# Latent attention's scores: rotary products over two heads at once from rounded high and low parts, and other tiles for the masks and maxima

## The chip, the cores and the metric

One core of a Trainium2 chip runs the whole program. The metric is the device time of one launch in microseconds (us); lower is better. A core has five engines that work side by side, each through its own list in order: PE (TensorE, matrix products; its weight loads are shown apart as PEld), DVE (VectorE), ACT (ScalarE), POOL (GpSimd) and SP (SyncE, which here starts transfers). They meet only by waiting on semaphores.

## The reference, cut to what matters

The kernel computes two layers of a decoder trunk over 256 positions (two blocks of 128). Each layer mixes four head groups, gates them, projects and normalises. The group that the change touches is latent attention with a rotary part:

```python
def _mla(c_q, c_kv, k_pe, ...):       # 4 heads
    q = (_rmsnorm(c_q, ...) @ w_uq)   # per head 128 plain + 64 rotary columns
    q = concat([q[..., :128], _rope(q[..., 128:], positions)])
    kv = (_rmsnorm(c_kv, ...) @ w_ukv)
    k_rot = _rope(k_pe, positions)    # one rotary key, shared by all heads
    k = concat([kv[..., :128], broadcast(k_rot)])
    return _causal_attention(q * (128 + 64) ** -0.5, k, v)   # mask, softmax, times v
```

So the scores of a head are a plain product over 128 features plus a rotary product over 64. All is float32, which PE takes in two ways: as float32, or from operands rounded to a format called fp32r. In the second way the kernel splits an operand into a rounded high part and the rest as a low part, and adds three products: high by high, low by high, high by low.

## The kernel before

**The stream.** Most of the work is a stream of weight tiles, 128 rows by 512 columns, numbered per layer by slot t. For each, SP loads two tiles at a time into `raw`; ACT writes the high part `hi` (L1073); DVE writes the low part `lo` = raw minus hi (L1414); PE multiplies: four 512-wide products with `hi` (L1327, L1328), then a wait for `lo`, then two with `lo` (L1331). `hi` and `lo` are rings of 5 places: a tile is split once PE has used the tile five slots before. A pair of raw tiles is loaded once `lo` of the pair four pairs earlier is written. Slots 144 to 159 are the chunk `rk`, 160 to 175 `rv`, 176 to 191 `z0`.

**The steps.** All else is hung between tiles by hand-written tables, `PE_AT`, `ACT_AT` and `DVE_AT`. A step at slot t runs on its engine right after that engine's own part of tile t, in the order in which the tables were filled. An engine that waits or works in a step keeps its next tile waiting. The steps that matter here, in the kernel before:

- PE, slot 156: `mla_scores` of heads 0 to 3. Per head four float32 products, for query block 0 (128 keys) and block 1 (256 keys) one plain (L1232) and one rotary (L1233). Each float32 product shows in the trace as two records.
- DVE, slots 161, 164, 173, 176: `mla_max` of a head: it adds the causal mask (L1807, 128x384), takes the two maxima (L1810, L1811) and scales them (L1812). Slots 165, 168, 177, 180: `mla_norm` (L1817, L1820). Slots 166, 169, 178, 181: `turn_head` (L1538), a transpose in 32x32 squares.
- ACT, slots 163, 166, 175, 178: `mla_exp` (L941) of a head, from DVE's maxima.
- DVE also has at 162 and 168 `cellT` (L1773, four 128-wide operations each), at 170 and 171 `rope_rk` of the two position blocks (L1783, L1784, L1800, 128x512 each), at 174 the transpose of `rk` (L1631).
- ACT, slots 150 and 151: `qrT` and `kpeT` copy the turned rotary queries and keys to `qrT` and `krT`, whose other halves hold zeros so that a pair of heads can share an operand.

**PE's order** is thus fixed by the program; nothing moves at run time but the moments.

Of the kernel before, what the change touches and what calls it, by code (L numbers as in the profile page):

```python
# [130 lines left out]
def _put(table, slot, *step):  # L131
    table.setdefault(slot, []).append(step)
# [30 lines left out]
for _h in range(HEADS):  # L163
    _put(ACT_AT, (78, 82, 88, 94)[_h], "mem_exp", _h)
    _put(ACT_AT, (102, 103, 110, 111)[_h], "mem_pT", _h)
    _put(ACT_AT, (163, 166, 175, 178)[_h], "mla_exp", _h)
for _s, *_step in [
# [29 lines left out]
for _h in range(HEADS):  # L197
    _put(DVE_AT, (76, 80, 86, 92)[_h], "mem_max", _h)
    _put(DVE_AT, (80, 84, 90, 96)[_h], "mem_norm", _h)
    _put(DVE_AT, (81, 85, 93, 97)[_h], "turn_head", "mem", _h)  # L200
    _put(DVE_AT, (103, 104, 111, 112)[_h], "lo", "mem_pT", _h)
    _put(DVE_AT, (161, 164, 173, 176)[_h], "mla_max", _h)
    _put(DVE_AT, (165, 168, 177, 180)[_h], "mla_norm", _h)
    _put(DVE_AT, (166, 169, 178, 181)[_h], "turn_head", "mla", _h)
for _s, *_step in [
        (20, "memv", 0), (22, "memv", 1),
        (36, "turn", "memk"), (211, "turn", "z3"), (228, "turn", "z2"), (45, "joined", "lx", 0), (53, "joined", "lx", 1),
        (61, "joined", "cq", 0), (69, "joined", "cq", 1),
        (237, "joined", "z1_", 0), (245, "joined", "z1_", 1),
        (110, "mem_out", 0), (118, "mem_out", 1),  # L210
        (123, "lo", "wukv", 0), (125, "lo", "wukv", 1), (128, "lo", "ckvT", 0),
        (54, "lo", "memk", 0), (56, "lo", "memk", 1), (63, "lo", "cq", 0), (71, "lo", "cq", 1),
        (86, "rms", 0), (88, "ckv", 0), (89, "kpe_rope", 0),
        (87, "gate_turn", 0), (95, "gates", 0), (99, "gate_scan", 0), (100, "gate_scan", 1), (101, "gate_scan", 2), (113, "ones", 0), (105, "gate_squares", 0),
        (102, "rms", 1), (107, "cqn", 0), (108, "cqn", 1), (109, "turn", "c"), (120, "cT", 0), (122, "cT", 1),
        (112, "ml_gap", 0), (113, "ml_gap", 1), (119, "ml_gap", 2), (120, "ml_gap", 3),
        (117, "ml_weigh", 0), (118, "ml_weigh", 1), (124, "ml_weigh", 2), (126, "ml_weigh", 3), (126, "skip", 0),
        (127, "ml_out", 0), (128, "ml_out", 1), (132, "ml_out", 2), (134, "ml_out", 3),
        (136, "cell_gate", 0), (137, "cell_gate", 1), (139, "cell_stats", 0), (140, "cell_stats", 1),
        (142, "cell_norm", 0), (144, "cell_norm", 1), (145, "turn", "cell"),  # L220
        (137, "q_rope", 0), (138, "q_rope", 1), (139, "turn_rotary", 0),
        (162, "cellT", 0), (168, "cellT", 1),
        (148, "rope_rq", 0), (150, "rope_rq", 1), (152, "turn", "rq"),
        (170, "rope_rk", 0), (171, "rope_rk", 1), (174, "turn", "rk"),
        (194, "mla_out", 0), (204, "mla_out", 1),
        (193, "ret_weigh", 0), (195, "ret_weigh", 1), (203, "ret_weigh", 2), (205, "ret_weigh", 3),
        (206, "ret_stats", 0), (208, "ret_norm", 0), (212, "ret_stats", 1), (214, "ret_norm", 1), (215, "ret_gate", 0), (216, "turn", "ret"),
        (229, "gate", 3, 0), (230, "gate", 3, 1), (242, "gate", 2, 0), (243, "gate", 2, 1),
        (244, "gate", 1, 0), (248, "gate", 1, 1),
        (232, "y_lo", 0), (233, "y_lo", 1), (235, "y_lo", 2), (237, "y_lo", 3),  # L230
        (246, "y_lo", 4), (247, "y_lo", 5), (252, "y_lo", 6), (253, "y_lo", 7)]:
    _put(DVE_AT, _s, *_step)
# [82 lines left out]
def build_trunk(nc, a, out):  # L315
    ctx = ExitStack()
    with ctx:
        def sb(name, shape, dt=F32):
            return ctx.enter_context(nc.sbuf_tensor(name, shape, dt))

        def signal(name, per_layer, before=0, step=1):
            return Signal(ctx.enter_context(nc.semaphore(name)), per_layer, before, step)
# [32 lines left out]
        gcol, freq = sb("gcol", [P, 4, HEADS]), sb("freq", [P, FR + FM])  # L355
        B, Br = zip(*(row_of[i] for i in range(10)))
        qr = sb("qr", [P, NT, HEADS * ROT])
        qrT = sb("qrT", [P, 2, SEQ])
        krr = sb("krr", [P, NT, P])
        krT = sb("krT", [P, 2, SEQ])  # L360
        prob = sb("prob", [P, 2, 512])
        pTl = sb("pTl", [P, 2, 512], F32R)
        with nc.sbuf_tensor("pTh", [P, 2, 512], F32R) as pTh:
# [137 lines left out]
        normed = signal("normed", 0)  # L501
        x_hi, x_lo = signal("x_hi", 8), signal("x_lo", 8)
        y_hi, y_lo = signal("y_hi", 8), signal("y_lo", 8)
        kv_split, uq_split = signal("kv_split", 3), signal("uq_split", 4)
        hi_part = signal("hi_part", len(HI_STEPS))
        conv_done, xc_done = signal("conv_done", 1), signal("xc_done", 2)
        lx_pad = signal("lx_pad", 1)
# [315 lines left out]
        def _(act):  # L823
# [20 lines left out]
            for l in range(DEPTH):  # L844
# [172 lines left out]
                def kpeT(_):  # L1017
                    wait_turned(act, l, "rot")
                    for r in range(2):
                        half_ = slice(r * ROT, (r + 1) * ROT)  # L1020
                        m = act.activation(krT[half_, r, :].rearrange("p (i a r) -> p i a r", i=NT, a=4),
                                           rot_blocks[half_, 4:6], ACT.Copy)
                    m.then_inc(rotary_turned.sem, 1)

# [69 lines left out]
        def _(pe):  # L1094
# [5 lines left out]
            for l in range(DEPTH):  # L1100
# [122 lines left out]
                def mla_scores(h):
                    if h == 0:
                        wait_read(pe, l, ("mla_kn", 0), ("mla_kn", 1), ("mla_qn", 0), ("mla_qn", 1))
                        pe.wait_ge(rotary_turned.sem, rotary_turned.at(l, 1))
                        pe.wait_ge(ready.sem, 3)
                        stand_alone(pe)
                    o = take("mla_scores", h)
                    for i, (c0, c1) in enumerate(((0, P), (P, TRI))):  # L1230
                        q = slice(i * P, (i + 1) * P)
                        pe.matmul(o[:, c0:c1], qnT[:, h, q], knT[:, h, 0:c1 - c0], start=True, stop=False)  # L1232
                        m = pe.matmul(o[:, c0:c1], qrT[:, h // 2, q], krT[:, h % 2, 0:c1 - c0], start=False, stop=True)  # L1233
# [154 lines left out]
        def _(dve):  # L1388
            dve.memset(tmp[:, 0:P], 1.0).then_inc(ready.sem, 1)
            dve.memset(half[:, :], -0.5).then_inc(ready.sem, 1)  # L1390
            dve.memset(krT[ROT:P, 0, :], 0.0)
            dve.memset(krT[0:ROT, 1, :], 0.0).then_inc(ready.sem, 1)
            for p in range(2):
                dve.sem_inc(acc_read[p].sem, 2)
            for b in range(NBANK):
# [40 lines left out]
            for l in range(DEPTH):  # L1436
# [88 lines left out]
                def turn_head(name, h):  # L1525

                    dve.wait_ge(prob_done.sem, prob_done.at(l, h + (HEADS if name == "mla" else 0)))
                    if (name, h) == ("mem", 0):
                        wait_job(dve, l, ("ml_fold", 0))
                    group = f"{name}{h // 2}"  # L1530
# [273 lines left out]
                def mla_max(h):

                    wait_job(dve, l, ("mla_scores", h))
                    dve.tensor_tensor(prob[:, h % 2, 0:TRI], bank(l, ("mla_scores", h))[:, 0:TRI], tri, ALU.add)\  # L1807
                       .then_inc(free_bank(l, "mla_scores", h), 1)
                    wait_read(dve, l, ("mla_scores", h))
                    dve.tensor_reduce(nmax[:, h % 2, 0:1], prob[:, h % 2, 0:P], AX.X, ALU.max, negate=True)  # L1810
                    link(dve.tensor_reduce(nmax[:, h % 2, 1:2], prob[:, h % 2, P:TRI], AX.X, ALU.max, negate=True))  # L1811
                    dve.tensor_scalar(nmax[:, h % 2, :], nmax[:, h % 2, :], MLA_SCALE, None, ALU.mult)\  # L1812
                       .then_inc(max_done.sem, 1)
# [64 lines left out]
                def residual(c, *only):  # L1878
# [8 lines left out]
                    for i in only or range(NT):  # L1887
# [166 lines left out]
```

## Time and profile before

| | us |
|---|---|
| median of 3 runs | 891.05 (890.68 to 891.11) |
| the profiled execution | 892.54 |
| its span, first to last instruction | 890.7 |
| PE busy (TensorE, 4532 instructions) | 883.3, 99% |
| DVE busy | 661.7, 74% |
| ACT busy | 487.7, 55% |
| granted TensorE clock, mean | 1.000 (2.4 GHz) |

A product on PE is pipelined: its row in the timeline lasts longer than the distance to the next start, so the work is read from starts, not from durations. Short operations on DVE and ACT overlap a little in the same way. A number in square brackets at the end of a timeline row is the idle time before it, with what ended it.

### The profile page before, as it was taken

How to read it: one execution, taken by the hardware profiler on the slowest of the kernel's cores; microseconds unless marked ns; L12 is line 12 of the kernel's file. 1: busy time of each engine (PE TensorE's matmuls, PEld its weight loads, DVE VectorE, ACT ScalarE, POOL GpSimd, SP SyncE). 2: the span in 40 equal slices, each digit the busy share in tenths (PEclk: the TensorE clock that was granted, in tenths of full speed). 3: DMA queues.
4: the chain of work that ended last, by engine and by line, in shares of the span. 5: the costliest groups of instructions: out<-in, count | busy, mean ns of one | idle time of the engine just before them, and what ended most of it. 6: DMA issues, size and time to landing. Idle time of an engine off the chain costs nothing.

```text
span 890.7 us, 13196 instructions
## 1 busy us (share of the span) xinstructions
PE 883.3 (99%) x4532; PEld 758.4 (85%) x4532; DVE 661.7 (74%) x1322; ACT 487.7 (55%) x914; POOL 18.0 (2%) x18
## 2 busy tenths in 40 slices
PE   9999999999999999999999999999999999999997
PEld 7888998788888888888888889888888888888896
DVE  6869697777595667766668887878777978777765
ACT  6656776445455346544476557746354553565541
POOL 0000000000000000000000000000000001000001
PEclk9999999999999999999999999999999999999999
DMA  9796587547669688666665965885485874978832
GB/s 358 283 326 210 137 264 247 185 143 216 217 212 319 213 243 271 192 198 196 193 192 173 312 243 155 280 267 157 145 267 154 272 236 153 289 209 265 322 95 95
DMA packets 70962, 198.23 MB, mean 223 GB/s; under 512 B 9448, under 2 KB 23024, under 8 KB 70256
## 3 DMA queue, kind: packets, MB, share of 16 engines
q1 hardware_dynamic: 70320, 196.34, 68.6%
q10 hardware_dynamic: 576, 1.05, 0.4%
q8 instruction: 36, 0.59, 0.3%
q14 instruction: 30, 0.25, 0.1%
HBM read 182.38 MB, written 14.95 MB: 222 GB/s over the span
## 4 chain that ended last, share of the span: by engine, by line
PE 92%; DMA 3%; issue 1%; DVE 1%; SPq 1%; ACT 1%; POOL 0%; POOLq 0%; ACTq 0%; DVEq 0%
PE acc L1327 23%; PE acc L1328 23%; PE acc L1331 23%; PE acc L1342 10%; PE acc L1348 5%; DMA B<-turn 1%; PE work L1116 1%; PE work L1115 1%; PE work L1114 1%; DMA raw<-in_w 1%; DMA turn<-B 1%; DMA B<-in_mem_t 1%; PE work L1233 1%; PE work L1232 1%; SPq L761 1%
## 5 line engine op out<-in xcount | busy, mean ns | idle before, releaser
L1414 DVE TENSOR_TENSOR lo<-raw,hi 128x512 fp32r<-128x512 f32 (+2 forms) x607 | 387.8, 656 | 185.5 <-ACT hi L1073 177.0
L1073 ACT ACTIVATE hi<-raw 128x512 fp32r<-128x512 f32 (+2 forms) x607 | 355.7, 603 | 295.3 <-PE acc L1331 229.5
L1327 PE MATMUL acc<-hi,xx 128*128 128x512 f32 (+2 forms) x768 | 285.6, 375 | 1.0 <-ACT hi L1073 1.0
L1328 PE MATMUL acc<-hi,xx 128*128 128x512 f32 (+2 forms) x768 | 283.6, 372 | 0.0
L1331 PE MATMUL acc<-lo,xx 128*128 128x512 f32 (+2 forms) x768 | 223.0, 372 | 0.0
L1327 PEld LDWEIGHTS acc<-hi,xx 128*128 128x128 f32 x768 | 144.6, 188 | 25.0 <-ACT hi L1073 1.4
L1328 PEld LDWEIGHTS acc<-hi,xx 128*128 128x128 f32 x768 | 144.6, 188 | 23.6
L1331 PEld LDWEIGHTS acc<-lo,xx 128*128 128x128 f32 x768 | 140.4, 188 | 24.6
L1342 PE MATMUL acc<-xx,hi 128*128 128x512 f32 x384 | 96.1, 392 | 0.0
L1342 PEld LDWEIGHTS acc<-xx,hi 128*128 128x128 f32 x384 | 69.3, 189 | 12.6
L1348 PEld LDWEIGHTS acc<-xx,lo 128*128 128x128 f32 x384 | 52.4, 190 | 3.7
L1348 PE MATMUL acc<-xx,lo 128*128 128x256 f32 x384 | 53.5, 282 | 0.0
L1327 PE MATMUL acc<-hi,mm 128*128 128x512 f32 x126 | 49.5, 393 | 0.6 <-DVE mm L1420 0.6
L1328 PE MATMUL acc<-hi,mm 128*128 128x512 f32 x126 | 49.1, 389 | 0.0
L1331 PE MATMUL acc<-lo,mm 128*128 128x512 f32 x126 | 38.8, 389 | 0.0
L1327 PEld LDWEIGHTS acc<-hi,mm 128*128 128x128 f32 x126 | 23.7, 188 | 5.7 <-DVE mm L1420 1.0
L1331 PEld LDWEIGHTS acc<-lo,mm 128*128 128x128 f32 x126 | 23.7, 188 | 5.0
L1328 PEld LDWEIGHTS acc<-hi,mm 128*128 128x128 f32 x126 | 23.7, 188 | 4.7
L799 POOL TENSOR_TENSOR rstd<-stats,half 128x4 f32<-128x4 f32 (+1 forms) x6 | 9.6, 1593 | 351.0 <-DVE stats L1842 221.6
L976 ACT ACTIVATE B<-work 128x512 f32<-128x512 f32 x12 | 7.2, 596 | 14.7 <-PE work L1116 14.7
L941 ACT ACTIVATE prob<-prob,nmax 128x128 f32<-128x128 f32 (+1 forms) x16 | 7.2, 448 | 10.3 <-DVE nmax L1812 10.3
L1580 DVE SCALAR_TENSOR_TENSOR B<-B,cols 128x256 f32<-128x256 f32 x24 | 11.6, 483 | 0.6
(345 smaller groups left out, 967.5 us busy)
## 6 DMA issues: line engine op xcount, KB each, us to landing
raw<-in_w SPq DMA_DIRECT2D x263, 512.0 KB, 4.4
B<-turn SPq DMA_DIRECT2D x80, 128.0 KB, 4.4
raw<-in_w SPq DMA_DIRECT2D x26, 256.0 KB, 2.7
turn<-B SPq DMA_DIRECT2D x12, 512.0 KB, 6.0
raw<-in_w SPq DMA_DIRECT2D x16, 328.0 KB, 3.3
turn<-Y SPq DMA_DIRECT2D x8, 512.0 KB, 5.4
Y<-in_wuq SPq DMA_DIRECT2D x2, 1152.0 KB, 8.7
Y<-in_x_t SPq DMA_DIRECT2D x4, 512.0 KB, 8.3
```

The source lines that it names most:

```text
L761: sp.dma_start(turn_to[name][b * 32:(b + 1) * 32, :].rearrange("c (a n) -> c a n", a=4), a["turn"][TURNS.index(name), :, b * n:(b + 1) * n ...
L799: return pool.tensor_tensor(dst, src, half[:, 0:n], ALU.pow)
L1073: act.activation(place(l, t, hi), raw[:, s, (t % 2) * w:(t % 2 + 1) * w], ACT.Copy)\
L1114: pe.matmul(o, ah, bh, start=start, stop=False)
L1115: pe.matmul(o, al, bh, start=False, stop=False)
L1327: pe.matmul(o, ah[:, q], hi[:, s, 0:w], start=k == 0, stop=False, skip_group_check=name == "memv")
L1328: pe.matmul(o, al[:, q], hi[:, s, 0:w], start=False, stop=False, skip_group_check=name == "memv")
L1331: m = pe.matmul(acc[:, p, i, 0:w], ah[:, i * P:(i + 1) * P], lo[:, s, 0:w], start=False, stop=k == KT - 1, skip_group_check=name == "memv")
L1342: pe.matmul(acc[:, p, j, :], hi[:, (l * SLOTS + t + u) % RING, q], x, start=k + u == 0 and kk == 0, stop=False, skip_group_check=True)
L1348: m = pe.matmul(acc[:, p, j, 0:SEQ], lo[:, s, q], both_parts[:, 2 * k + kk, 0, :], start=False, stop=2 * k + kk == KT - 1, skip_group_chec ...
L1414: dve.tensor_tensor(place(l, t, lo), raw[:, s, (t % 2) * w:(t % 2 + 1) * w], place(l, t, hi).bitcast(F32), ALU.subtract).then_inc(lo_done. ...
L1580: m = dve.scalar_tensor_tensor(xcT[:, j, :], LX[:, j, tap:tap + SEQ], wcol, xcT[:, j, :], ALU.mult, ALU.add)
```

## The change

Five things, each in both layers:

- The rotary operands become fp32r pairs: ACT's copies write `qrh` (in the buffer `pTh`) and `krh`, and a new DVE step `rot_lo` at slot 153 writes the low parts `qrl` (in `pTl`) and `krl`.
- PE's rotary products take two heads at once. A bank of PSUM now holds two heads of one query block instead of one head of two blocks: per bank three fp32r products, 256 wide for block 0 and 512 wide for block 1. Then the plain products follow, float32 as before.
- `mla_max` works on a bank, so on two heads of one block: mask and maxima, and after the second block the scaling of both heads.
- The tables move: `mla_max` from 161, 164, 173, 176 to 161, 162, 170, 171; `mla_exp` from 163, 166, 175, 178 to 164, 166, 172, 174; `mla_norm` from 165, 168, 177, 180 to 166, 168, 174, 177; the transposes to 167, 169, 175, 178.
- Two more memsets at the start, and three waits: `qrT` for an old job, `turn_head` of head 2 for the transpose of `rk`, `mla_max` 2 for the transposes of heads 0 and 1.

```diff
-    _put(ACT_AT, (163, 166, 175, 178)[_h], "mla_exp", _h)
+    _put(ACT_AT, (164, 166, 172, 174)[_h], "mla_exp", _h)
-    _put(DVE_AT, (161, 164, 173, 176)[_h], "mla_max", _h)
+    _put(DVE_AT, (161, 162, 170, 171)[_h], "mla_max", _h)
...
+(153, "rot_lo", 0),
...
+                        pe.wait_ge(kv_split.sem, kv_split.at(l, 3))
...
+                        for b in range(HEADS):
+                            (q, i), o = divmod(b, 2), take("mla_scores", b)
+                            w = (i + 1) * P
+                            o = o[:, 0:2 * w].rearrange("p (h k) -> p h k", h=2)
+                            (ah, al), (bh, bl) = (... qrh, qrl), (... krh, krl)
+                            pe.matmul(o, ah, bh, start=True, stop=False, skip_group_check=True)
+                            pe.matmul(o, al, bh, start=False, stop=False, skip_group_check=True)
+                            pe.matmul(o, ah, bl, start=False, stop=False, skip_group_check=True)
...
+                    for h in (2 * q, 2 * q + 1):
+                        m = pe.matmul(o[:, h % 2 * w:(h % 2 + 1) * w], qnT[:, h, i * P:(i + 1) * P], knT[:, h, 0:w],
+                                      start=False, stop=True, skip_group_check=True)
...
+                def rot_lo(_):
+                    dve.wait_ge(rotary_turned.sem, rotary_turned.at(l, 1))
+                    wait_job(dve, l, ("mla_v", 1))
+                    dve.tensor_tensor(at(qrl), rot_blocks[:, 0:4], at(qrh).bitcast(F32), ALU.subtract)
+                    for r in range(2):
+                        m = dve.tensor_tensor(at(krl), rot_blocks[half_, 4:6], at(krh).bitcast(F32), ALU.subtract)
+                    m.then_inc(kv_split.sem, 1)
...
+                def mla_max(n):
+                    i, c0, c1 = n % 2, n % 2 * P, P + n % 2 * 2 * P
+                    wait_job(dve, l, ("mla_scores", n))
+                    dve.tensor_tensor(prob[:, :, c0:c1], o, tri[:, c0:c1]..., ALU.add)
+                    link(dve.tensor_reduce(nmax[:, :, i], prob[:, :, c0:c1], AX.X, ALU.max, negate=True))
+                    if i:
+                        for h in range(2):
+                            dve.tensor_scalar(nmax[:, h, :], nmax[:, h, :], MLA_SCALE, None, ALU.mult)
```

On PE, at the end of slot 156, stood before (the first two heads of four; `B` are the plain operands, `acc` rows are the stream):

```order
L1232 MATMUL work<-B 128x128
L1233 MATMUL work<-krT,qrT 128x128
L1232 MATMUL work<-B 128x256
L1233 MATMUL work<-krT,qrT 128x256
L1232 MATMUL work<-B 128x128
L1233 MATMUL work<-krT,qrT 128x128
L1232 MATMUL work<-B 128x256
L1233 MATMUL work<-krT,qrT 128x256
```

and stands now (the first two banks' rotary products, which come twice, then all the plain ones):

```order
L1235 MATMUL work<-krh,pTh 128x256
L1236 MATMUL work<-krh,pTl 128x256
L1237 MATMUL work<-krl,pTh 128x256
L1235 MATMUL work<-krh,pTh 128x512
L1236 MATMUL work<-krh,pTl 128x512
L1237 MATMUL work<-krl,pTh 128x512
...
L1242 MATMUL work<-B 128x128 x2
L1242 MATMUL work<-B 128x256 x2
```

Eight float32 rotary products became twelve fp32r ones; the plain ones only moved behind them.

On DVE, from tile 170 on, stood before (`lo` is the low part of a tile, `Y` and `tmp` with `cos` and `sin` the steps `rope_rk`, `prob` and `nmax` the step `mla_max`):

```order
L1414 TENSOR_TENSOR lo<-raw,hi 128x512
L1783 TENSOR_TENSOR Y<-acc,cos 128x512
L1784 TENSOR_TENSOR tmp<-acc,sin 128x512
L1800 TENSOR_TENSOR Y<-Y,tmp 128x512
L1414 TENSOR_TENSOR lo<-raw,hi 128x512
L1783 TENSOR_TENSOR Y<-acc,cos 128x512
L1784 TENSOR_TENSOR tmp<-acc,sin 128x512
L1800 TENSOR_TENSOR Y<-Y,tmp 128x512
L1414 TENSOR_TENSOR lo<-raw,hi 128x512 x2
L1807 TENSOR_TENSOR prob<-work,const 128x384
```

and stands now:

```order
L1426 TENSOR_TENSOR lo<-raw,hi 128x512
L1837 TENSOR_TENSOR prob<-work,const 128x2x128
L1840 TENSOR_REDUCE nmax<-prob 128x2
L1797 TENSOR_TENSOR Y<-acc,cos 128x512
...
L1426 TENSOR_TENSOR lo<-raw,hi 128x512
L1837 TENSOR_TENSOR prob<-work,const 128x2x256
L1840 TENSOR_REDUCE nmax<-prob 128x2
L1843 TENSOR_SCALAR nmax<-nmax 128x2 x2
L1797 TENSOR_TENSOR Y<-acc,cos 128x512
...
L1426 TENSOR_TENSOR lo<-raw,hi 128x512 x3
```

The masks and maxima of heads 2 and 3 moved ahead of the two `rope_rk` steps, so they now stand between the low parts of tiles 170 and 172.

On ACT, around the exponentials of latent attention, stood before (`hi` is the high part of a tile, `prob,rsum` the step `mla_exp`):

```order
L1073 ACTIVATE hi<-raw 128x512 x12
L941 ACT_TABLE_LOAD
L941 ACTIVATE prob,rsum<-prob,nmax 128x128
L941 ACTIVATE prob,rsum<-prob,nmax 128x256
L1073 ACTIVATE hi<-raw 128x512 x3
L941 ACTIVATE prob,rsum<-prob,nmax 128x128
L941 ACTIVATE prob,rsum<-prob,nmax 128x256
L1073 ACTIVATE hi<-raw 128x512 x9
```

and stands now:

```order
L1075 ACTIVATE hi<-raw 128x512 x13
L942 ACT_TABLE_LOAD
L942 ACTIVATE prob,rsum<-prob,nmax 128x128
L942 ACTIVATE prob,rsum<-prob,nmax 128x256
L1075 ACTIVATE hi<-raw 128x512 x2
L942 ACTIVATE prob,rsum<-prob,nmax 128x128
L942 ACTIVATE prob,rsum<-prob,nmax 128x256
L1075 ACTIVATE hi<-raw 128x512 x6
```

The first exponential moved one tile later, behind `hi` of tile 164; the third came from behind tile 175 to behind tile 172.

## Rows read from the trace of the kernel before

**Rows 1.** PE's waits over the span: who for whom, us, times, longest.
```profile
PE acc L1327 <- ACT hi L1073: 1.0, 1, 1.0
```

**Rows 2.** PE's timeline, slots 156 and 157, then 172: start us, us, work.
```profile
227.74 0.62 PE L1331 MATMUL acc<-lo,xx 128*128 128x512 f32 x2
228.19 0.38 PE L1232 MATMUL work<-B 128*128 128x128 f32 x2
...
228.63 0.60 PE L1232 MATMUL work<-B 128*128 128x256 f32 x2
229.07 0.59 PE L1233 MATMUL work<-krT,qrT 128*128 128x256 f32 x2
229.50 0.38 PE L1232 MATMUL work<-B 128*128 128x128 f32 x2
...
234.35 0.62 PE L1331 MATMUL acc<-lo,xx 128*128 128x512 f32 x2
...
254.75 0.62 PE L1331 MATMUL acc<-lo,xx 128*128 128x512 f32 x2
```

**Rows 3.** PE's timeline, 18 fp32r products 256 wide, and the next.
```profile
186.21 0.28 PE L1114 MATMUL work<-Xr 128*128 128x256 f32 x1
...
188.36 0.40 PE L1327 MATMUL acc<-hi,xx 128*128 128x512 f32 x1
```

**Rows 4.** DVE's timeline, slots 153 to 172 of layer 1.
```profile
220.30 1.86 DVE L1414 TENSOR_TENSOR lo<-raw,hi 128x512 fp32r<-128x512 f32 x3
...
235.73 0.69 DVE L1414 TENSOR_TENSOR lo<-raw,hi 128x512 fp32r<-128x512 f32 x1 [4.62 <-ACT hi L1073]
...
240.46 0.55 DVE L1807 TENSOR_TENSOR prob<-work,const 128x384 f32<-128x384 f32 x1
...
241.25 0.41 DVE L1811 TENSOR_REDUCE nmax<-prob 128x1 f32<-128x256 f32 x1
241.69 0.17 DVE L1812 TENSOR_SCALAR nmax<-nmax 128x2 f32<-128x2 f32 x1
...
244.13 1.25 DVE L1414 TENSOR_TENSOR lo<-raw,hi 128x512 fp32r<-128x512 f32 x2
...
247.61 0.57 DVE L1538 STREAM_TRANSPOSE Y<-prob 128x384 f32<-128x384 f32 x1
248.10 0.66 DVE L1414 TENSOR_TENSOR lo<-raw,hi 128x512 fp32r<-128x512 f32 x1
248.68 0.69 DVE L1783 TENSOR_TENSOR Y<-acc,cos 128x512 f32<-128x512 f32 x1
...
250.72 0.69 DVE L1414 TENSOR_TENSOR lo<-raw,hi 128x512 fp32r<-128x512 f32 x1
...
253.37 1.29 DVE L1414 TENSOR_TENSOR lo<-raw,hi 128x512 fp32r<-128x512 f32 x2
```

**Rows 5.** ACT's timeline, slots 162 to 166.
```profile
235.06 0.63 ACT L1073 ACTIVATE hi<-raw 128x512 fp32r<-128x512 f32 x1 [6.04 <-PE acc L1331]
...
237.01 1.28 ACT L941 ACT_TABLE_LOAD   x1
...
239.20 1.14 ACT L1073 ACTIVATE hi<-raw 128x512 fp32r<-128x512 f32 x2
240.50 0.63 ACT L1073 ACTIVATE hi<-raw 128x512 fp32r<-128x512 f32 x1 [0.16 <-PE acc L1331]
```

**Rows 6.** The tile `nmax`: durations in ns, min, median, max.
```profile
L1544 DVE TENSOR_REDUCE nmax<-work x8: 680/682/685, 101.6 to 559.0; 128x2 f32<-128x512 f32 x8
```

**Rows 7.** ACT's and PE's timelines where PE waits for a high part.
```profile
165.04 1.13 ACT L1073 ACTIVATE hi<-raw 128x512 fp32r<-128x512 f32 x2
...
165.71 0.50 PE L1327 MATMUL acc<-hi,xx 128*128 128x512 f32 x1 [1.02 <-ACT hi L1073]
166.05 0.40 PE L1328 MATMUL acc<-hi,xx 128*128 128x512 f32 x1
```

**Rows 8.** DVE's timeline, slot 172 of layer 2.
```profile
691.04 1.29 DVE L1414 TENSOR_TENSOR lo<-raw,hi 128x512 fp32r<-128x512 f32 x2
```

More of the change, by code:

```diff
@@ L201 @@
     _put(DVE_AT, (103, 104, 111, 112)[_h], "lo", "mem_pT", _h)
-    _put(DVE_AT, (161, 164, 173, 176)[_h], "mla_max", _h)
-    _put(DVE_AT, (165, 168, 177, 180)[_h], "mla_norm", _h)
-    _put(DVE_AT, (166, 169, 178, 181)[_h], "turn_head", "mla", _h)
+    _put(DVE_AT, (161, 162, 170, 171)[_h], "mla_max", _h)
+    _put(DVE_AT, (166, 168, 174, 177)[_h], "mla_norm", _h)
+    _put(DVE_AT, (167, 169, 175, 178)[_h], "turn_head", "mla", _h)
 for _s, *_step in [
@@ L222 @@
         (162, "cellT", 0), (168, "cellT", 1),
-        (148, "rope_rq", 0), (150, "rope_rq", 1), (152, "turn", "rq"),
+        (148, "rope_rq", 0), (150, "rope_rq", 1), (152, "turn", "rq"), (153, "rot_lo", 0),
         (170, "rope_rk", 0), (171, "rope_rk", 1), (174, "turn", "rk"),
@@ L357, in build_trunk @@
         qr = sb("qr", [P, NT, HEADS * ROT])
-        qrT = sb("qrT", [P, 2, SEQ])
+        krl = sb("krl", [P, 2, SEQ], F32R)
         krr = sb("krr", [P, NT, P])
-        krT = sb("krT", [P, 2, SEQ])
+        krh = sb("krh", [P, 2, SEQ], F32R)
         prob = sb("prob", [P, 2, 512])
@@ L409, in build_trunk @@
         ckvp = pTl[:, 0, 0:SEQ], pTl[:, 0, SEQ:2 * SEQ]
+        qrh, qrl = (x[:, 0, :] for x in (pTh, pTl))
         gap = Y[:, 4096 - 2 * TRI:4096].rearrange("p (b c) -> p b c", b=2)
@@ L503, in build_trunk @@
         y_hi, y_lo = signal("y_hi", 8), signal("y_lo", 8)
-        kv_split, uq_split = signal("kv_split", 3), signal("uq_split", 4)
+        kv_split, uq_split = signal("kv_split", 4), signal("uq_split", 4)
         hi_part = signal("hi_part", len(HI_STEPS))
@@ L1020, in kpeT @@
                         half_ = slice(r * ROT, (r + 1) * ROT)
-                        m = act.activation(krT[half_, r, :].rearrange("p (i a r) -> p i a r", i=NT, a=4),
+                        m = act.activation(krh[half_, r, :].rearrange("p (i a r) -> p i a r", i=NT, a=4),
                                            rot_blocks[half_, 4:6], ACT.Copy)
@@ L1030, in qrT_ @@
                     wait_turned(act, l, "rot")
-                    act.activation(qrT[:, :, :].rearrange("p j (i a r) -> p (j i) a r", i=NT, a=4), rot_blocks[:, 0:4], ACT.Copy)\
+                    wait_job(act, l, ("ml_out", HEADS - 1))
+                    act.activation(qrh.rearrange("p (n a r) -> p n a r", n=4, a=4), rot_blocks[:, 0:4], ACT.Copy)\
                        .then_inc(rotary_turned.sem, 1)
@@ L1221, in mla_v, with mla_scores @@
                             both(wukvp, lambda x: x[:, :, 1, :])).then_inc(job_done.sem, 1)
[L1223 to L1226, printed above, removed]
+                def mla_scores(n):
+                    if n == 0:
+                        pe.wait_ge(kv_split.sem, kv_split.at(l, 3))
                         pe.wait_ge(ready.sem, 3)
                         stand_alone(pe)
[L1229 to L1233, printed above, removed]
+                        for b in range(HEADS):
+                            (q, i), o = divmod(b, 2), take("mla_scores", b)
+                            w = (i + 1) * P
+                            o = o[:, 0:2 * w].rearrange("p (h k) -> p h k", h=2)
+                            (ah, al), (bh, bl) = (x[:, q * SEQ + i * P:q * SEQ + (i + 1) * P] for x in (qrh, qrl)),                                                  (x[:, :, 0:w] for x in (krh, krl))
+                            pe.matmul(o, ah, bh, start=True, stop=False, skip_group_check=True)
+                            pe.matmul(o, al, bh, start=False, stop=False, skip_group_check=True)
+                            pe.matmul(o, ah, bl, start=False, stop=False, skip_group_check=True)
+                        wait_read(pe, l, ("mla_kn", 0), ("mla_kn", 1), ("mla_qn", 0), ("mla_qn", 1))
+                    (q, i), o = divmod(n, 2), bank(l, ("mla_scores", n))
+                    w = (i + 1) * P
+                    for h in (2 * q, 2 * q + 1):
+                        m = pe.matmul(o[:, h % 2 * w:(h % 2 + 1) * w], qnT[:, h, i * P:(i + 1) * P], knT[:, h, 0:w],
+                                      start=False, stop=True, skip_group_check=True)
                     m.then_inc(job_done.sem, 1)
@@ L1390, in _ @@
             dve.memset(half[:, :], -0.5).then_inc(ready.sem, 1)
-            dve.memset(krT[ROT:P, 0, :], 0.0)
-            dve.memset(krT[0:ROT, 1, :], 0.0).then_inc(ready.sem, 1)
+            for part in (krl, krh):
+                dve.memset(part[ROT:P, 0, :].bitcast(F32), 0.0)
+                m = dve.memset(part[0:ROT, 1, :].bitcast(F32), 0.0)
+            m.then_inc(ready.sem, 1)
             for p in range(2):
@@ L1527, in turn_head @@
                     dve.wait_ge(prob_done.sem, prob_done.at(l, h + (HEADS if name == "mla" else 0)))
+                    if (name, h) == ("mla", 2):
+                        dve.wait_ge(squared["rk"].sem, squared["rk"].at(l, 0))
                     if (name, h) == ("mem", 0):
@@ L1802, in rope_ret @@
                     return go
[L1804 to L1813, printed above, removed]
+                def rot_lo(_):
+                    dve.wait_ge(rotary_turned.sem, rotary_turned.at(l, 1))
+                    wait_job(dve, l, ("mla_v", 1))
+                    at = lambda x: x.rearrange("p (n a r) -> p n a r", n=4, a=4)
+                    dve.tensor_tensor(at(qrl), rot_blocks[:, 0:4], at(qrh).bitcast(F32), ALU.subtract)
+                    for r in range(2):
+                        half_ = slice(r * ROT, (r + 1) * ROT)
+                        at = lambda x: x[half_, r, :].rearrange("p (i a r) -> p i a r", i=NT, a=4)
+                        m = dve.tensor_tensor(at(krl), rot_blocks[half_, 4:6], at(krh).bitcast(F32), ALU.subtract)
+                    m.then_inc(kv_split.sem, 1)
@@ new lines, in mla_max @@
+                def mla_max(n):
+                    i, c0, c1 = n % 2, n % 2 * P, P + n % 2 * 2 * P
+                    wait_job(dve, l, ("mla_scores", n))
+                    if n == 2:
+                        dve.wait_ge(squared["mla0"].sem, squared["mla0"].at(l, 1))
+                    o = bank(l, ("mla_scores", n))[:, 0:2 * (c1 - c0)].rearrange("p (h k) -> p h k", h=2)
+                    dve.tensor_tensor(prob[:, :, c0:c1], o, tri[:, c0:c1].unsqueeze(1).to_broadcast([P, 2, c1 - c0]), ALU.add)\
+                       .then_inc(free_bank(l, "mla_scores", n), 1)
+                    wait_read(dve, l, ("mla_scores", n))
+                    link(dve.tensor_reduce(nmax[:, :, i], prob[:, :, c0:c1], AX.X, ALU.max, negate=True))
+                    if i:
+                        for h in range(2):
+                            dve.tensor_scalar(nmax[:, h, :], nmax[:, h, :], MLA_SCALE, None, ALU.mult)\
+                               .then_inc(max_done.sem, 1)
@@ L1897, in _ @@
                          "q_rope": q_rope, "rope_rq": rope_ret("rq", rqt, 0), "rope_rk": rope_ret("rk", rkt, 2),
-                         "mla_max": mla_max, "mla_norm": mla_norm, "mla_out": out_pair("mla_out", mlao),
+                         "rot_lo": rot_lo, "mla_max": mla_max, "mla_norm": mla_norm, "mla_out": out_pair("mla_out", mlao),
                          "ret_weigh": ret_weigh, "ret_stats": ret_stats, "ret_norm": ret_norm,
```

## The prediction

> **What bounds the kernel now.** First the list of waits: PE is busy 99% of the span, and it waits for another engine inside the layers once, 1.0 us [rows 1]. So every microsecond of PE's own list is a microsecond of the kernel, and work on DVE and ACT costs nothing until it makes PE wait. Then PE's timeline: a tile of the stream has six 512-wide products and starts every 1.36 us (tile 157's low products start at 234.35, tile 172's, 15 tiles on, at 254.75: 20.40 / 15) [rows 2]. Then the same tiles on DVE: the low part of tile 172 starts at 253.37 and lasts 0.69, so it is written at 254.06 against a need at 254.75 [rows 2, 4]. Here DVE is 0.69 us ahead of PE, no more; from 244.13 to 253.37 it runs one operation behind another. In layer 2 the same row stands 437.67 us later [rows 8], so one walk serves for both layers.
>
> **What PE saves.** The block at slot 156 takes 234.35 - 227.74 - 1.36 = 5.25 us [rows 2]. A 128-wide float32 product takes half of 228.63 - 228.19, so 0.22, and a 256-wide one 0.44 (228.63 to 229.07 the plain one, to 229.50 the rotary one) [rows 2]. The rotary half, four of each, is 4 x 0.655 = 2.62 us, and goes. In come six fp32r products 256 wide and six 512 wide. The first kind takes (188.36 - 186.21) / 18 = 0.119 us [rows 3], the second 1.36 / 6 = 0.227. That is 0.72 + 1.36 = 2.08. Saved per layer: 0.54 us, for both 1.08. The block becomes 4.71 us. The plain products keep their number, shape and kind, so I cost their move at nothing; changes between the two kinds of product cost nothing to be seen before, since 4 x 1.31 already fills the block.
>
> On the 256-wide product the row shows 0.119 us. The Trainium skill ("TensorE: Matmul & The Clock Gate", section on the back-to-back issue gap) gives width / 2.4 + 2.5 ns, 109 ns for this width, where only the products count; the trace does not agree by 10 ns. By that rule the estimate would be a saving 0.06 us larger per layer.
>
> **What is added and hidden.** `rot_lo` after tile 153's low part: three subtractions, at most 0.69 for the 512-wide one and 0.42 for each of the others, 1.5 us. Tile 153's low part starts at 220.30 [rows 4], so the step ends by 222.5, and tile 154's low part by 223.2. PE needs that at 227.74 - 2 x 1.36 = 225.02 and the new operands at 228.19. Both are covered by about 2 us or more; without that cover it would cost up to 1.5 us a layer. The two memsets stand in DVE's first microseconds, while it waits for the first tiles. ACT's copies keep their shapes. SP's list is the same.
>
> **The schedule after slot 156.** PE's times are now 0.54 earlier: low products of tile 157 at 233.81, of tile 172 at 254.21. DVE must be followed up to there.
>
> ACT sets where it starts. Before, `hi` of tile 162 runs at 235.06 and of tile 166 at 240.50, each as PE frees a place of the ring, 1.36 a tile [rows 5]. So `hi` of 164 would run at 235.06 + 2 x 1.36 = 237.78 before, 237.24 now. Behind it now come the table load and the first exponential: 2.19 from 237.01 to 239.20 [rows 5], less the load's 1.28 gives 0.91 for an exponential alone. So: `hi` 164 at 237.24, table load at 237.89 (0.65 later, as before), `hi` 165 at 240.08, 166 and the second exponential about 0.53 apart, and 0.91 later `hi` 167 at 242.04. Its low part follows 0.67 later, as 235.73 follows 235.06 [rows 4, 5]: tile 167 on DVE at 242.71. DVE's own list alone would bring it there at 242.6, so the start is held from two sides.
>
> From there DVE does not rest. Before, 244.13 to 248.10 is tile 167, tile 168, norm, `cellT`, tile 169, transpose: 3.97 [rows 4]. The same six follow now, with one more transpose in between (247.61 to 248.10, 0.49), then tile 170's low part (0.58): 242.71 + 3.97 + 0.49 + 0.58 = 247.75. Before, that point was 248.68 [rows 4], which is 248.14 on PE's new clock. So DVE is 0.39 better off here, because one `mla_max` has moved into the idle time ahead of tile 163.
>
> Now the moved steps. `mla_max` 2: a mask of 256 elements and a reduce of 256. The mask of 384 takes 0.55, the 512-wide operation from PSUM 0.69, so 256 takes 0.42, plus 0.03 to the dependent one; the reduce of 256 takes 0.44 start to start [rows 4]. Sum 0.89: 248.64. `rope_rk` 0 takes 250.72 - 248.68 = 2.04 [rows 4]: 250.68. Tile 171: 0.61, 251.29. `mla_max` 3: mask of 512, 0.69 + 0.03; reduce of 512; two scalings, 0.17 each, overlapping by 0.1 as neighbours do here, 0.16 or more. The trace has no reduce of 512 from SBUF. From below the 256-wide row, 0.41; from above 0.90, twice 0.44 [rows 4]; I take the 512-wide reduce from PSUM, 0.68 [rows 6], plus 0.02. Sum 1.58: 252.87. `rope_rk` 1: 254.91. Tile 172's low part lasts 0.69: written at 255.60.
>
> PE needs it at 254.21. When PE really waits, it loses a little more: the high part at 165.04 takes 0.62 and ends at 165.66, yet the product behind the waiting one starts at 166.05, so the waiting one ran from 165.82, 0.16 after the operand [rows 7]. So tile 172's low products run at 255.76: **a wait of 1.55 us in each layer.**
>
> Behind it nothing else is late. Tiles 173 and 174 follow at 0.6, written by 256.8; norm 0.65, transpose of `rk` 1.17 (1.24 long), and tile 175 is written near 259.3, with PE's need at 255.76 + 3 x 1.36 = 259.84. ACT waits for the maxima until 252.9, runs the third exponential, and has `hi` of 173 at 254.4; PE needs it at 256.2. The wait is behind `hi` 173 and 174 only.
>
> On the reduce the row shows 0.68 from PSUM, and the subtraction from SBUF takes 0.69, the operation from PSUM at 248.68 the same 0.69 [rows 4]. The Trainium skill ("VectorE: DVE Perf Modes", section on the errata) gives 58 cycles plus the width for a source in SBUF and 120 for one in PSUM, at 0.96 GHz: 0.59 us for the new reduce. The trace does not agree with that difference. By the rule the estimate of the wait would be about 0.1 us shorter in each layer, the sign of the result the same.
>
> **The sum.** Per layer -0.54 + 1.55 = +1.01; both layers +2.0. The profiled execution has 892.54 us around a span of 890.7; its changed counterpart comes to 892.7 in span and 894.6 in all. The median of the runs is 1.49 below the profiled execution; on it, 891.05 + 2.0 = **893.1 us**. The reduce alone moves this by -0.6 to +0.4 (its bounds, twice), and the point where DVE starts its dense stretch by 0.2 either way per layer.
>
> A change of 0.2%, 1.8 us, is what a measurement can tell; the edges are 889.3 and 892.8.
>
> **Rivals.**
>
> *Only the saving shows.* DVE's low part of tile 172 comes in time, and the kernel takes 891.05 - 1.08 = 890.0. For it: PE's block is sure to shrink, and the new form does less mask work over a layer (2.5 for two heads against 2 x 1.31). Against it: DVE had 0.69 us before tile 172 and now has about 2.5 us of masks and maxima before it that stood after it, less the 0.39 + 0.54 gained. And even if tile 172 were in time, tile 175 comes with norm and transpose behind it at 259.3 against 258.29, so about 1 us of wait would come there. Chance 8%, and within 0.2%. Faster by more than 0.2% needs another 0.7 us saved by PE; 4%.
>
> *The wait is there but smaller,* by DVE operations that overlap more than their rows before (0.1 us each at ten joints). Then the wait is 0.9 to 1.4 us, and the time 891.8 to 892.8, within 0.2%. Chance 22%.
>
> *A second wait.* ACT stands still for the maxima up to tile 172's exponential, so `hi` of tiles 173 and 174 and behind them the reloads of `raw` come late. That decides from the point where DVE's scaling ends after 254.7 (then `hi` 173 is written after 256.2). Then every further 0.1 on DVE costs PE 0.1, and with the reload's transfer late too it would be about 1 us a layer more: 895. By the walk there is 1.8 us of room. Chance 5%.
>
> *The change does not do what it says:* the rotary products at fp32r cost more than read, for instance 256-wide at the 512-wide price, 6 x 0.11 = 0.65 a layer. Then nothing is saved and the time is 894.4. Against it stand 18 such products in a row at 0.119 [rows 3]. Chance 4%.
>
> The forecast itself, 892.8 to 893.7, has the rest, 57%. Faster 0.04; same 0.08 + 0.22 = 0.30; slower 0.66. Range 891.7 to 894.1: it leaves out the first rival and the dearest ones.
>
> **What would show it.** In the changed profile: the time from the last low product of tile 156 to tile 157's low products shrinks by 0.54; twelve rows of `krh`/`krl` at 0.12 and 0.23. A new wait of PE at a low product (L1341) for DVE, once in each layer, about 1.4 to 1.6 us, some 27.5 us after the block begins. DVE without idle time for the 13 us before it. ACT idle about 3.5 us for `nmax` before the third exponential. Wrong would be: no wait at tile 172, the wait at another tile, or one for ACT or a transfer.

## The result, and the profile after

| | before | changed |
|---|---|---|
| median | 890.91 us (890.53 to 891.88, 12 runs) | 892.76 us (892.58 to 894.01, 12 runs) |
| profiled execution, its span | 892.54, 890.7 | 892.74, 890.9 |

The ratio is 1.0023, with a 95% interval of 1.0015 to 1.0030: the change made the kernel slower by 1.85 us (1.3 to 2.7). The forecast was 893.1 in a range of 891.7 to 894.1, with 0.66 on slower by more than 0.2%. The ratio measured lies just past that edge of 1.002, and its interval reaches below it: that the kernel became slower is clear, that it became slower by more than 0.2% is not.

**The new wait.** The list of PE's waits in the changed kernel (who for whom: us in total, times, longest) answers to [rows 1]:

```profile
PE acc L1341 <- DVE lo L1426: 2.5, 2, 1.3
PE work L1100 <- DVE half L1400: 1.1, 1, 1.1
PE acc L1313 <- ACT hi L1067: 0.5, 1, 0.5
PE acc L1393 <- ACT tmp L1087: 0.3, 1, 0.3
```

The first row is new: twice, once in each layer, PE stands at low products until DVE has written the low part of a tile. All others are at the program's start and end. The row's 1.3 us is less than what PE loses, since a product's row reaches on into the wait. The starts tell it better. PE's timeline around the block and at tile 172 answers to [rows 2]:

```profile
225.84 0.61 PE L1341 MATMUL acc<-lo,xx 128*128 128x512 f32 x2
226.30 0.28 PE L1235 MATMUL work<-krh,pTh 128*128 128x256 f32 x1
226.41 0.28 PE L1236 MATMUL work<-krh,pTl 128*128 128x256 f32 x1
226.53 0.28 PE L1237 MATMUL work<-krl,pTh 128*128 128x256 f32 x1
226.65 0.40 PE L1235 MATMUL work<-krh,pTh 128*128 128x512 f32 x1
226.88 0.40 PE L1236 MATMUL work<-krh,pTl 128*128 128x512 f32 x1
...
228.40 2.78 PE L1242 MATMUL work<-B 128*128 128x128 f32 x16
...
231.94 0.62 PE L1341 MATMUL acc<-lo,xx 128*128 128x512 f32 x2
...
252.11 0.39 PE L1338 MATMUL acc<-hi,xx 128*128 128x512 f32 x1
253.77 0.73 PE L1341 MATMUL acc<-lo,xx 128*128 128x512 f32 x2 [1.27 <-DVE lo L1426]
254.34 0.40 PE L1337 MATMUL acc<-hi,xx 128*128 128x512 f32 x1
```

The block: 231.94 - 225.84 - 1.36 = 4.74 us, against 5.25 before, so 0.51 saved. Rotary products start every 0.12 us (256 wide) and 0.23 us (512 wide). The wait: tile 172 is the fifteenth after tile 157, and its low products were due at 231.94 + 15 x 1.36 = 252.34. They started at 253.77, and since the next product comes 0.57 later where two take 0.455, they ran from 253.88: 1.54 us lost. In layer 2 the same pair of starts, 690.85 and 692.50, gives 1.53.

DVE's timeline before that wait answers to [rows 4] (`x3` in a row are three tiles' operations put together):

```profile
240.78 0.69 DVE L1426 TENSOR_TENSOR lo<-raw,hi 128x512 fp32r<-128x512 f32 x1
...
245.26 0.65 DVE L1426 TENSOR_TENSOR lo<-raw,hi 128x512 fp32r<-128x512 f32 x1
245.83 0.41 DVE L1837 TENSOR_TENSOR prob<-work,const 128x256 f32<-128x256 f32 x1
246.28 0.42 DVE L1840 TENSOR_REDUCE nmax<-prob 128x2 f32<-128x256 f32 x1
246.73 0.69 DVE L1797 TENSOR_TENSOR Y<-acc,cos 128x512 f32<-128x512 f32 x1
...
248.78 0.69 DVE L1426 TENSOR_TENSOR lo<-raw,hi 128x512 fp32r<-128x512 f32 x1
249.39 0.68 DVE L1837 TENSOR_TENSOR prob<-work,const 128x512 f32<-128x512 f32 x1
250.11 0.69 DVE L1840 TENSOR_REDUCE nmax<-prob 128x2 f32<-128x512 f32 x1
250.83 0.24 DVE L1843 TENSOR_SCALAR nmax<-nmax 128x2 f32<-128x2 f32 x2
250.98 0.68 DVE L1797 TENSOR_TENSOR Y<-acc,cos 128x512 f32<-128x512 f32 x1
...
253.02 1.90 DVE L1426 TENSOR_TENSOR lo<-raw,hi 128x512 fp32r<-128x512 f32 x3
```

No row from 240.78 to 253.02 carries idle time. Tile 172's low part starts at 253.02 and is written at 253.71; PE's weight load for the waiting product starts at 253.77.

**Why the two spans differ by 0.2 only.** The profiled execution of the kernel before had a wait that this one has not: PE for a high part at 165.71 [rows 1, 7]. By its starts that cost 1.29 us; the program's start took the rest. So PE stood 1.89 us earlier here (226.30 against 228.19) before anything of the change had run. The source of that wait is a transfer (into the buffer `B`) that a step on DVE waited for:

```profile
163.23 0.69 DVE L1687 TENSOR_TENSOR B<-B,cols 128x512 f32<-128x512 f32 x1 [2.77 <-DMA B<-turn]
```

ACT then waited for DVE's result before it could write the next high part. This wait comes and goes. In the profiles where DVE waited for that transfer 2.8, 2.8, 2.5, 2.4 and 2.0 us in one layer, PE lost 1.29, 1.34, 1.06, 0.88 and 0.54 us by its starts; where it waited 1.5 us or less, PE lost nothing there. The profiles of the kernel before and of its variant below have it, and three of the seven profiles of the changed kernel and its variants. The execution profiled before was 1.6 us above its median, this one is at its median. So the medians carry the result, and the profiles the mechanism: 2 x (1.54 - 0.51) = 2.1 us, against 1.85 between the medians. The 0.2 us between the two are not explained; the interval of 1.3 to 2.7 us holds both.

### The profile page after: what moved, and what is told of

Same layout as the page of the kernel before. It is cut to its first block, busy times and chain, and to the rows that moved or that the text cites. A ratio compares the mean times of both kernels' runs of the same rounds, so it can differ in the third digit from the quotient of the medians.

```text
span 890.9 us, 13190 instructions
## 1 busy us (share of the span) xinstructions
PE 882.2 (99%) x4524; PEld 756.8 (85%) x4524; DVE 665.0 (75%) x1322; ACT 488.4 (55%) x914; POOL 18.0 (2%) x18
## 4 chain that ended last, share of the span: by engine, by line
PE 94%; DVE 3%; issue 1%; ACT 1%; DMA 0%; POOL 0%; POOLq 0%; ACTq 0%; DVEq 0%
PE acc L1341 23%; PE acc L1337 23%; PE acc L1338 23%; PE acc L1352 10%; PE acc L1358 5%; PE work L1118 1%; PE work L1117 1%; PE work L1116 1%; DVE lo L1426 1%; PE work L1242 1%; DMA B<-in_mem_t 0%; PE work L1111 0%; PE work L1265 0%; PE work L1254 0%; PE work L1174 0%
## 5 line engine op out<-in xcount | busy, mean ns | idle before, releaser
L1338 PE MATMUL acc<-hi,B1r 128*128 128x512 f32 (+1 forms) x32 | 12.0, 377 | 0.0
```

What stands on the lines that cost most here:

```text
L1338: pe.matmul(o, al[:, q], hi[:, s, 0:w], start=False, stop=False, skip_group_check=name == "memv")
```

## The experiments

All were timed against the kernel before on the same chip, whose median was 890.72 us for the first four and 890.94 for the other three.

**Masks and maxima of heads 2 and 3 late.** Only the tables differ from the changed kernel:

```diff
-    _put(ACT_AT, (164, 166, 172, 174)[_h], "mla_exp", _h)
+    _put(ACT_AT, (164, 166, 177, 178)[_h], "mla_exp", _h)
-    _put(DVE_AT, (161, 162, 170, 171)[_h], "mla_max", _h)
-    _put(DVE_AT, (166, 168, 174, 177)[_h], "mla_norm", _h)
-    _put(DVE_AT, (167, 169, 175, 178)[_h], "turn_head", "mla", _h)
+    _put(DVE_AT, (161, 162, 173, 175)[_h], "mla_max", _h)
+    _put(DVE_AT, (166, 168, 178, 180)[_h], "mla_norm", _h)
+    _put(DVE_AT, (167, 169, 179, 181)[_h], "turn_head", "mla", _h)
```

> The changed kernel with heads 2 and 3 late: mla_max at 173 and 175 instead of 170 and 171, mla_exp at 177 and 178, mla_norm at 178 and 180, the transposes at 179 and 181. Theory (the whole loss is PE's wait for the low part of tile 172, behind the moved masks and maxima): that wait is gone. By the walk on DVE, with PE's clock as in the prediction, the low part of tile 172 is written at 253.1 against a need at 254.05, tile 175 at 257.0 against 258.1, tile 176 at 259.15 against 259.5. What is left is PE's shorter block, 0.51 us a layer: 1.0 us under the kernel before, about 889.9, ratio 0.9989. Rival (the loss lies in the new products or in the subtractions of rot_lo, and the tables do nothing): as the changed kernel, 892.8.

Measured: 889.65 us (889.46 to 890.35, 11 runs), ratio 0.9987 (0.9978 to 0.9996). PE's waits in its profile are those at the start and the end alone:

```profile
PE work L1100 <- DVE half L1400: 1.1, 1, 1.1
PE acc L1393 <- ACT tmp L1087: 0.3, 1, 0.3
PE acc L1313 <- ACT hi L1067: 0.3, 1, 0.3
```

What is left is PE's saving, 1.07 us. With the time of `rot_lo` twice below this is the lowest, ahead of both kernels; the rival that laid the loss on the new products falls.

**The tables alone.** The kernel before, its own products and its `mla_max` by head, with heads 2 and 3 at the change's slots, and two waits to keep shared buffers in order:

```diff
-    _put(ACT_AT, (163, 166, 175, 178)[_h], "mla_exp", _h)
-    _put(DVE_AT, (161, 164, 173, 176)[_h], "mla_max", _h)
-    _put(DVE_AT, (165, 168, 177, 180)[_h], "mla_norm", _h)
-    _put(DVE_AT, (166, 169, 178, 181)[_h], "turn_head", "mla", _h)
+    _put(ACT_AT, (163, 166, 172, 174)[_h], "mla_exp", _h)
+    _put(DVE_AT, (161, 164, 170, 171)[_h], "mla_max", _h)
+    _put(DVE_AT, (165, 168, 174, 177)[_h], "mla_norm", _h)
+    _put(DVE_AT, (166, 169, 175, 178)[_h], "turn_head", "mla", _h)
```

> The kernel before with its own products, masks and maxima by head, but with heads 2 and 3 at the slots of the changed kernel: mla_max 170 and 171, mla_exp 172 and 174, mla_norm 174 and 177, the transposes 175 and 178. Theory: DVE reaches tile 170 as before; two mla_max of 1.32 us now stand ahead of tile 172. Low part written at 248.68 + 2 x (1.32 + 2.04) + 0.61 + 0.69 = 256.7, plus 0.16 to the product, against 254.75: a wait of 2.1 us in each layer, 4.2 us over the kernel before, about 895.1, ratio 1.0047. Rival (tables do nothing): 890.9.

Measured: 896.72 us (896.63 to 897.17, 5 runs), ratio 1.0065 (1.0053 to 1.0078), 6.0 us over the kernel before. The direction and the place were right, the size was 1.8 us short. PE's timeline in layer 1:

```profile
253.26 0.39 PE L1328 MATMUL acc<-hi,xx 128*128 128x512 f32 x1
255.48 1.04 PE L1331 MATMUL acc<-lo,xx 128*128 128x512 f32 x2 [1.82 <-DVE lo L1414]
256.31 0.63 PE L1327 MATMUL acc<-hi,xx 128*128 128x512 f32 x1
256.74 0.63 PE L1328 MATMUL acc<-hi,xx 128*128 128x512 f32 x1
257.17 0.63 PE L1327 MATMUL acc<-hi,xx 128*128 128x512 f32 x1
257.59 0.63 PE L1328 MATMUL acc<-hi,xx 128*128 128x512 f32 x1
258.02 1.05 PE L1331 MATMUL acc<-lo,xx 128*128 128x512 f32 x2
258.87 0.51 PE L1327 MATMUL acc<-hi,xx 128*128 128x512 f32 x1
259.23 0.40 PE L1328 MATMUL acc<-hi,xx 128*128 128x512 f32 x1
```

The wait is 255.59 - (253.26 + 0.23) = 2.1 us, as expected. But behind it eight products take 3.39 us, 0.42 each instead of 0.227, and the ninth 0.36. That stretch by engine (us, PE busy (x), granted clock, DMA share, GB/s):

```profile
255.48:258.87 3.39, 3.39 (x8) 0.53 0.58 195
```

The granted clock fell to half, the level of 1.2 GHz. Summed over the stretch this costs 1.6 us. In layer 2 of the same execution the wait was as long, and the clock stayed. So 2 x 2.1 + 1.6 = 5.8 of the 6.0 us. All five executions had a mean clock of 0.997 or 0.998, where those of the kernel before had 0.999 or 1.000, so the fall came in each of them.

**The last reduce twice.** In `mla_max`, for the last bank only:

```diff
                     link(dve.tensor_reduce(nmax[:, :, i], prob[:, :, c0:c1], AX.X, ALU.max, negate=True))
+                    if n == 3:
+                        link(dve.tensor_reduce(nmax[:, :, i], prob[:, :, c0:c1], AX.X, ALU.max, negate=True))
```

> The changed kernel with the last reduce of mla_max (heads 2 and 3, second block, 512 elements) run twice, once per layer more. Theory: the second one, 0.72 us from start to start, goes whole into PE's wait at tile 172, which grows from 1.55 to 2.27 us: 1.4 us over the changed kernel, about 894.2, ratio to the kernel before 1.0038. Rival (DVE is not what PE waits for at that place, or has room): as the changed kernel, 892.8.

Measured: 895.78 us, but spread from 894.31 to 897.67 over 5 runs, ratio 1.0056 (1.0043 to 1.0070). The wait behaved as said: in layer 2 the products before it and after it are

```profile
694.10 0.39 PE L1338 MATMUL acc<-hi,xx 128*128 128x512 f32 x1
696.46 0.74 PE L1341 MATMUL acc<-lo,xx 128*128 128x512 f32 x2 [1.98 <-DVE lo L1426]
```

so 696.57 - 694.33 = 2.24 us, 0.7 more than in the changed kernel. In layer 1 the half clock came again (granted clock 0.52 from 254.39 to 257.88) and took 1.6 us:

```profile
254.39 1.22 PE L1341 MATMUL acc<-lo,xx 128*128 128x512 f32 x2 [1.98 <-DVE lo L1426]
255.41 0.63 PE L1337 MATMUL acc<-hi,xx 128*128 128x512 f32 x1
```

The lowest run, 894.31, is what DVE's time alone gives (894.2); the others lie 1.4 to 3.4 above it. The mean clock of each execution goes with this: 0.999 in the lowest, 0.997 in the three at 895.67 to 896.73, and 0.995 in the one at 897.67, which is what a fall in both layers would give; that execution has no timeline.

**The last masks and maxima one slot later.**

```diff
-    _put(ACT_AT, (164, 166, 172, 174)[_h], "mla_exp", _h)
-    _put(DVE_AT, (161, 162, 170, 171)[_h], "mla_max", _h)
+    _put(ACT_AT, (164, 166, 173, 174)[_h], "mla_exp", _h)
+    _put(DVE_AT, (161, 162, 170, 172)[_h], "mla_max", _h)
```

> The changed kernel with only its last mla_max and the third exponential one slot later (172 and 173). Theory, by the walk: tile 172's low part is written at 254.0, just in time (need 254.05), but the masks and maxima now hold tile 173: written at 256.2, plus 0.16, against 255.57, a wait of 0.8 us; behind it norm and transpose of rk hold tile 175: 259.4 against 259.1, 0.3 us more. Sum 1.1 us a layer instead of 1.55: 2 x (1.1 - 0.51) = 1.2 us over the kernel before, about 892.1, ratio 1.0013. A reading in which the place alone decides (behind tile 172 is free): 889.9. Rival (tables do nothing): 892.8.

Measured: 893.92 us (893.73 to 894.82, 6 runs), ratio 1.0033 (1.0020 to 1.0045): slower than the changed kernel, where I expected it faster. PE's timeline:

```profile
253.42 0.62 PE L1341 MATMUL acc<-lo,xx 128*128 128x512 f32 x2
...
254.57 0.40 PE L1338 MATMUL acc<-hi,xx 128*128 128x512 f32 x1
255.43 0.73 PE L1341 MATMUL acc<-lo,xx 128*128 128x512 f32 x2 [0.47 <-DVE lo L1426]
256.31 0.50 PE L1337 MATMUL acc<-hi,xx 128*128 128x512 f32 x1
...
258.51 0.40 PE L1338 MATMUL acc<-hi,xx 128*128 128x512 f32 x1
259.42 0.73 PE L1341 MATMUL acc<-lo,xx 128*128 128x512 f32 x2 [0.52 <-DVE lo L1426]
```

Tile 172 (253.42) is in time and tile 173 late by 0.76, both as the walk had it. Then comes what it missed: tile 174's first product (256.31) runs 0.43 late, waiting for its high part, and the list of PE's waits does not show it. ACT stood at the third exponential, and wrote it late:

```profile
254.75 0.40 ACT L942 ACTIVATE prob<-prob,nmax 128x128 f32<-128x128 f32 x1 [5.49 <-DVE nmax L1843]
...
255.64 0.61 ACT L1075 ACTIVATE hi<-raw 128x512 fp32r<-128x512 f32 x1
```

DVE in turn waited 0.91 us for that high part, and tile 175 came 0.79 late where I had 0.3. The sum is 0.76 + 0.43 + 0.79 = 1.98 us a layer, and 2 x (1.98 - 0.51) = 2.9 of the measured 3.2.

**`rot_lo` twice,** on top of the late masks: its three subtractions in a loop of two, with a wait between.

```diff
+                    for again in range(2):
                         dve.tensor_tensor(at(qrl), rot_blocks[:, 0:4], at(qrh).bitcast(F32), ALU.subtract)
...
+                        if again == 0:
+                            link(m)
```

> The kernel of the run before with the late masks, with the subtractions of rot_lo run twice, one after the other: about 1.5 us more of DVE work at slot 153 in each layer. Theory (rot_lo is wholly hidden, with about 2 us of room before tile 154's low part and 5 before the products that use it): no wait of PE there, the time of late_masks, 889.7. Rival (rot_lo is on the path, or near it): up to 3 us more, 892.7.

Measured: 889.66 us (889.40 to 889.82, 11 runs), the time of the late masks to 0.01. Once, the step takes 1.48 us on DVE in the changed kernel (218.98 to 220.46), and even twice it is hidden: PE has no wait in the layers of that profile.

**Exponentials late, masks where the change put them.**

```diff
-    _put(ACT_AT, (164, 166, 172, 174)[_h], "mla_exp", _h)
-    _put(DVE_AT, (166, 168, 174, 177)[_h], "mla_norm", _h)
-    _put(DVE_AT, (167, 169, 175, 178)[_h], "turn_head", "mla", _h)
+    _put(ACT_AT, (164, 166, 177, 178)[_h], "mla_exp", _h)
+    _put(DVE_AT, (166, 168, 178, 180)[_h], "mla_norm", _h)
+    _put(DVE_AT, (167, 169, 179, 181)[_h], "turn_head", "mla", _h)
```

> The changed kernel with its masks and maxima where the change put them (170, 171), but exponentials, norms and transposes of heads 2 and 3 late (ACT 177, 178; DVE 178, 180 and 179, 181). Theory (PE waits for DVE's low part of tile 172 alone, and ACT's standing still for the maxima is covered): the same wait of 1.55 us in each layer at tile 172, 892.6, ratio 1.0021. Rival (ACT's stop at tile 172 has a share in it): less than that, down to 889.7 if it is all.

Measured: 892.74 us (892.64 to 894.88, 11 runs), ratio 1.0020 (1.0012 to 1.0029): the changed kernel's time. PE's starts at tile 172 are 254.22 and 255.87, 1.65 apart, as the changed kernel's 1.66 (the profiled execution, the one at 894.88, also had two passing waits for a high part, 2.2 us together by its starts, earlier in layer 1). So ACT's stop has no share there, and it takes both this run and the one with all steps late to say that the masks alone made the wait.

**The last reduce three times,** the loop of the second run once more:

> The changed kernel with the last reduce of mla_max run three times. By DVE's time alone the wait at tile 172 becomes 1.55 + 2 x 0.72 = 2.99 us a layer and the time 890.7 - 1.0 + 6.0 = 895.7. New theory, from the two runs in which PE waited 2.1 and 2.27 us: behind a wait of that length the granted clock falls in some executions to the half, products take 0.43 us instead of 0.227 for about 3 us, which costs 1.6 us; with 3 us of wait it should fall in both layers, 895.7 + 3.2 = 898.9. Rival (the slow stretch was chance and not tied to the wait): 895.7 with a spread as before.

Measured: 900.38 us, six runs: 896.0, 896.86, 900.27, 900.48, 900.58, 900.68. PE's timeline in layer 2, then both slow stretches by engine (columns as above):

```profile
694.35 0.39 PE L1338 MATMUL acc<-hi,xx 128*128 128x512 f32 x1
697.44 1.22 PE L1341 MATMUL acc<-lo,xx 128*128 128x512 f32 x2 [2.70 <-DVE lo L1426]
698.46 0.63 PE L1337 MATMUL acc<-hi,xx 128*128 128x512 f32 x1
```

```profile
256.30:259.80 3.50, 3.50 (x10) 0.52 0.45 150
697.50:703.50 6.00, 6.00 (x14) 0.50 0.45 156
```

The wait is 3.0 us, as the walk says, and this time the clock fell in both layers, for 1.6 us of loss in the first and 2.9 in the second. That gives 895.7 + 4.5 = 900.2, and four runs are there, with mean clocks of 0.993 or 0.994. The run at 896.0 has 0.999, so no fall, and is near 895.7; the one at 896.86 has 0.997 and is 1.2 above it, so it had one. I had expected 898.9; the theory that a long wait brings the slow stretch holds, its price was too low.

## Why the prediction was right

- **PE's block:** 0.54 us saved were forecast, 0.51 measured in the profile, and 1.07 us in both layers by the run with late masks.
- **The additions hidden:** `rot_lo` took 1.48 us against 1.5, and doubling it cost nothing.
- **Where DVE starts its dense stretch:** tile 167 at 242.71 on the old clock, less the 1.89 us by which this execution was ahead, is 240.82; the row shows 240.78.
- **The moved steps:** `mla_max` 2 took 0.90 (forecast 0.89), `rope_rk` 2.05 (2.04), `mla_max` 3 1.59 (1.58), the uncertain reduce 0.69 (0.68; that price was a choice between bounds of 0.41 and 0.90, and the choice held). Tile 172's low part began at 253.02; 254.91 - 1.89 is the same.
- **The wait:** 1.55 forecast, 1.54 and 1.53 measured. The tables alone, one more reduce and two more put it at 2.1, 2.24 and 3.0 us, each as worked out from DVE's rows.
- **Nothing else late:** no other wait behind it, shown by the list of waits and by the exponentials' run.
- **The sum:** +2.0 forecast, +1.85 measured. The forecast of the profiled execution, 894.6, failed (892.74): I had taken a passing wait of the kernel before for a lasting one.
- **Two smaller things were off.** ACT stood idle 4.16 us for `nmax` before the third exponential, not 3.5; nothing waited for it. Neither it nor the next point enters the sum. By the width rule that the prediction cites from the Trainium skill ("TensorE: Matmul & The Clock Gate", section on the back-to-back issue gap) the estimate of 0.06 us counts the 256-wide products alone; the six 512-wide ones would add as much again.

**The rivals.** "Only the saving shows" is what the late masks give, so it was one table away. The second wait through ACT did not come in the changed kernel, but it did come one slot further on: ACT's stop for the maxima and DVE's order have to be walked together, and in that run's expectation I had walked DVE alone. The clock was no rival of mine at all. It explains the size of three experiments, and not the changed kernel's median: the profile has it at 1.0 throughout, and all twelve executions have a mean of 0.999 or 1.000. The one at 894.01 has 0.999 too, so it had no such stretch; 1.25 us above the median is the size of the passing wait, but no timeline of that execution shows it.

## What to carry to other kernels

Where one engine paces everything and the others keep ahead by less than a microsecond, ask of every moved step what stands behind it on its own engine and when the pacing engine needs that; here 2.5 us of masks crossed one tile with 0.7 us to spare, and took back three times what the arithmetic had saved. A step that waits holds the queue of its engine too, so a slot that is right for one engine can be wrong for the next. Before adding up, look whether the profiled execution stands at the median of the runs.

## What the runs showed of the hardware

A longer wait of PE cost more than its length in these runs, because the granted clock fell behind it. With waits of about 1.5 us, in the changed kernel and in the one with late exponentials, the clock was 1.0 in both layers of the profiles, and none of their 23 executions has a mean below 0.999. With 2.1 and 2.24 us it fell to half in the first layer and not in the second of the profiled executions, and with 3.0 us in both. Each fall took 1.6 to 2.9 us. By the mean clock it came in all five executions with waits of 2.1 us, in four of five with 2.24 us, and in five of six with 3.0 us, which is why the last run has two groups, near 896 with no fall or one and near 900 with two. Why the same wait brings it in one layer and not in the other, or in one execution and not in the next, no run here shows.

The Trainium skill ("TensorE: Matmul & The Clock Gate", the section on HAM oscillation) says that an idle PE brings the clock down and that the next work then starts slow. The trace agrees, with products at 0.43 us instead of 0.227; in one of the four slow stretches, that of layer 1 with three reduces, three products (255.66 to 256.46) still ran at the full clock before the slow ones.
